# Value products in split fp32r form, in groups of four heads, in the last loop of a two-block fp32 kernel

## The reference

```
u = rmsnorm_2(h); proj = u @ w_in
# 16 MLA heads (latent q and kv, rope) and 16 "fox" heads (forget gate), head size 64
s = q @ k.T * scale (+ cum[t] - cum[s] for fox), causal mask over 272 keys
p = softmax(s)                      # per head, 256 real query rows
out = einsum('bhqk,bhkd->bhqd', p, v)
o_mla * silu(z_mla) @ w_br_mla,  o_fox * silu(z_fox) @ w_br_fox
mixed = (sigmoid(gate_a) * y_mla + sigmoid(gate_b) * y_fox) @ w_out
h = h + rmsnorm_2(mixed)
```

## Time and profile before

| | us |
|---|---|
| median of 3 runs | 955.57 |
| profiled execution, whole | 956.61 |
| its span in the trace | 954.8 |
| PE busy | 930.5 (97%) |
| DVE busy | 580.2 (61%) |
| ACT busy | 479.3 (50%) |
| POOL busy | 38.8 (4%) |
| the last loop | about 647 to 899 |

### The profile page before, as it was taken

The page is one execution under the profiler, slowest core; times in us unless marked ns, Lnnn a source line. Parts: engine busy times, 40 slices in busy tenths (PEclk is TensorE's granted clock), DMA queues, the critical chain, the costliest instruction groups (busy, mean ns, idle before and its releaser), DMA issues.

```text
span 954.8 us, 13629 instructions
## 1 busy us (share of the span) xinstructions
PE 930.5 (97%) x5017; PEld 775.3 (81%) x5017; DVE 580.2 (61%) x1061; ACT 479.3 (50%) x773; POOL 38.8 (4%) x67
## 2 busy tenths in 40 slices
PE   6999999999999999999999999999999999999996
PEld 6877778888888899878888888889987878878775
DVE  5866857646355578567355453776665565565565
ACT  6565566344353547556353443686354445445442
POOL 1013200000000000000000000001011000000000
PEclk9999999999999999999999999999999999999998
DMA  8542256554635522236645546232433242433541
GB/s 304 213 177 89 93 190 220 196 201 147 238 142 213 184 89 90 89 131 242 223 152 199 196 153 238 94 134 80 189 101 127 100 161 89 177 132 132 174 158 44
DMA packets 26375, 150.43 MB, mean 158 GB/s; under 512 B 3664, under 2 KB 3920, under 8 KB 12112
## 3 DMA queue, kind: packets, MB, share of 16 engines
q1 hardware_dynamic: 24912, 147.44, 42.3%
q0 software_dynamic: 1408, 2.25, 0.8%
HBM read 148.50 MB, written 1.05 MB: 157 GB/s over the span
## 4 chain that ended last, share of the span: by engine, by line
PE 83%; DVE 8%; ACT 4%; DMA 2%; issue 2%; DVEq 1%; ACTq 0%; SPq 0%
PE bank L472 24%; PE bank L473 23%; PE bank L474 23%; DVE w_lo L1830 2%; DMA w_raw<-w_main_dram 2%; PE bank L543 1%; PE bank L1033 1%; PE bank L752 1%; DVE arena L2217 1%; PE bank L1048 1%; PE bank L1086 1%; PE bank L890 1%; PE bank L1068 1%; PE bank L1069 1%; PE bank L866 1%
## 5 line engine op out<-in xcount | busy, mean ns | idle before, releaser
L472 PE MATMUL bank<-w_hi,x_hi 128*128 128x512 f32 (+2 forms) x640 | 259.7, 406 | 1.3 <-DVE w_lo L1738 0.8
L473 PE MATMUL bank<-w_lo,x_hi 128*128 128x512 f32 (+2 forms) x640 | 249.9, 390 | 0.0
L474 PE MATMUL bank<-w_hi,x_lo 128*128 128x512 f32 (+2 forms) x640 | 249.5, 390 | 0.0
L1738 DVE TENSOR_TENSOR w_lo<-w_raw,w_hi 128x2048 fp32r<-128x2048 f32 x50 | 114.5, 2292 | 75.3 <-ACT w_hi L1219 74.3
L472 PEld LDWEIGHTS bank<-w_hi,x_hi 128*128 128x128 f32 x640 | 120.6, 188 | 30.0 <-issue 4.1
L474 PEld LDWEIGHTS bank<-w_hi,x_lo 128*128 128x128 f32 x640 | 120.2, 188 | 27.4
L1219 ACT ACTIVATE w_hi<-w_raw 128x2048 fp32r<-128x2048 f32 x54 | 103.4, 1918 | 76.9 <-DMA w_raw<-w_main_dram 70.9
L473 PEld LDWEIGHTS bank<-w_lo,x_hi 128*128 128x128 f32 x640 | 120.6, 188 | 22.3
L1830 DVE TENSOR_TENSOR w_lo<-w_raw,w_hi 128x2048 fp32r<-128x2048 f32 x51 | 116.2, 2284 | 5.0 <-ACT w_hi L1280 4.8
L1280 ACT ACTIVATE w_hi<-w_raw 128x2048 fp32r<-128x2048 f32 x50 | 94.8, 1906 | 14.6 <-DMA w_raw<-w_main_dram 14.1
L472 PE MATMUL bank<-x_hi,w_hi 128*128 128x256 f32 (+1 forms) x272 | 80.4, 296 | 9.0 <-DVE w_lo L1840 8.4
(11 more groups left out here) (372 smaller groups left out, 1460.4 us busy)
## 6 DMA issues: line engine op xcount, KB each, us to landing
w_raw<-w_main_dram SPq DMA_DIRECT2D x111, 1024.0 KB, 4.9
s_raw<-w_side_dram SPq DMA_DIRECT2D x51, 512.0 KB, 4.2
w_raw<-w_main_dram SPq DMA_DIRECT2D x2, 512.0 KB, 6.5
h<-x_dram SPq DMA_DIRECT2D x2, 512.0 KB, 10.7
arena<-rows_dram POOLq DMA_DIRECT2D x2, 512.0 KB, 4.1
arena<-x_t_dram SPq DMA_DIRECT2D x1, 768.0 KB, 7.0
out_dram<-arena SPq DMA_DIRECT2D x1, 512.0 KB, 2.6
out_dram<-arena SPq DMA_DIRECT2D x2, 256.0 KB, 2.1
```

What stands on the lines that cost most here:

```text
L472: pe.matmul(out, ah, bh, start=first, stop=False)
L473: pe.matmul(out, ah, bl, start=False, stop=False)
L474: return pe.matmul(out, al, bh, start=False, stop=last)
L1738: dve.tensor_tensor(w_lo[:, slot, 4 * g:4 * g + 4, :], w_raw[:, g, :, :], w_hi[:, slot, 4 * g:4 * g + 4, :], ALU.subtract).then_inc(w_lo_o ...
```

## The change

Each value product becomes two fp32r matmuls in place of one fp32 matmul. The transposed probabilities are split: ACT copies bank 5 to `hi` as fp32r, DVE writes `lo` = bank 5 - `hi`, in place of DVE's copy. GpSimd splits the 64 value columns of each head into `[v_hi | v_lo]`, side by side. One matmul takes `hi` against all 128 columns, one takes `lo` against the 64 of `v_hi`. A head now takes 128 columns of a bank, so a bank holds four heads (QUAD), and the meta turns, meta products and `group_out` come eight times, at n = 4, 8, 12, ..., 28 and 31; `group_out` first adds the two halves (`tensor_reduce`) and then scales. The meta product has 4 x 64 columns in place of 512.

The tiles of `hi` and `lo` lie in `s_hi`, `s_lo` for the MLA heads and in `g_hi`, `g_lo` for fox. So that these are free, the splits of the side units of `w_uq` move from the end of turns 1 and 5 to turns 4 and 8, between the new ACT copy and `head_exps(n + 2)` on ACT, and between the new subtraction and `head_masked(n + 2)` on DVE; `mla_query` of turns 5 and 9 goes behind the first rider half. `o_mla` moves to another place in SBUF, and some fox turns by one.

```diff
-FOX_TURNS = {RIDERS.index([("gb", 0, 1)]) + j: (2 * j, 2 * j + 1) for j in range(2)}
+FOX_TURNS = {RIDERS.index([("gb", 0, 1)]) + 2 * j: (2 * j, 2 * j + 1) for j in range(2)}
-GROUP_ENDS = {GROUP: 0, 2 * GROUP: 1, 3 * GROUP: 2, 2 * NH - 1: 3}
+QUAD = 4
+QUAD_ENDS = {QUAD * (g + 1) if g < 7 else 2 * NH - 1: g for g in range(8)}
...
+        def head_tiles(n):
+            if n >= NH:
+                return g_hi[:, 2 * P + M:5 * P + M], g_lo[:, M:3 * P + M], g_lo[:, 3 * P + M:5 * P + M].rearrange(...)
+            slot = 0 if 4 <= n < 8 else 1
+            return (s_hi[:, slot, 0:3 * P], s_lo[:, slot, 0:3 * P],
+                    s_hi[:, slot, 3 * P:5 * P].rearrange("p (k e) -> p k e", k=2))
...
# GpSimd
+            for n in range(2 * NH):
+                pool.wait_ge(pt_ps, A2 + n + 1)
...
+                v = (v_m if n < NH else f_v)[:, :, n % NH * HD:(n % NH + 1) * HD]
+                pair = head_tiles(n)[2]
+                hi, lo = pair[:, :, 0:HD], pair[:, :, HD:2 * HD]
+                pool.tensor_copy(hi, v)
+                pool.drain()
+                pool.tensor_tensor(lo, v, hi, ALU.subtract).then_inc(vs_ok, 1)
+                if n in (8, 9, 12, 13):
...
# PE
-                pe.matmul(bank[6][:, at], pt[:, 0:P], v(0), start=first, stop=False)
-                pe.matmul(bank[7][:, at], pt[:, P:2 * P], v(0), start=first, stop=False)
-                pe.matmul(bank[7][:, at], pt[:, 2 * P:3 * P], v(1), start=False, stop=False)
+                for b, i, kt in ((bank[6], 0, 0), (bank[7], 1, 0), (bank[7], 2, 1)):
+                    v_ = v[:, kt if n < NH else 1 - kt, :]
+                    pe.matmul(b[:, a:a + 2 * HD], hi[:, i * P:(i + 1) * P], v_, start=first and kt == 0, stop=False)
+                    pe.matmul(b[:, a:a + HD], lo[:, i * P:(i + 1) * P], v_[:, 0:HD], start=False, stop=False)
...
-                    ins = pe.matmul(bank[6 + r][:, :], pt[:, 384 + r * P:384 + (r + 1) * P], meta_v[g], start=False, stop=True)
+                    ins = pe.matmul(halves(bank[6 + r], 0), pt[:, 384 + r * P:384 + (r + 1) * P], meta_v[g], start=False, stop=True)
...
-                if n + 3 < NH:
+                if n + 3 < NH and n not in (5, 9):
                     mla_query(n + 3)
...
                     riders(RIDERS[n], 0)
+                if n in (5, 9):
+                    mla_query(n + 3)
# ACT
+                act.wait_ge(pt_ps, A2 + n + 1)
+                act.activation(head_tiles(n)[0], bank[5][:, 0:384], ACT.Copy).then_inc(ph_ok, 1)
+                if n in (4, 8):
+                    act.wait_ge(uq_ps, n + 1)
+                    split_side(U_Q + 1 + n // 4)
...
                 if n + 2 < NH or n in FOX_PAIRS:
                     head_exps(n + 2)
-                if n in GROUP_ENDS and n < 2 * NH - 1:
-                    meta_turned(GROUP_ENDS[n])
+                if n in QUAD_ENDS and n < 2 * NH - 1:
+                    meta_turned(QUAD_ENDS[n])
...
-                if n in (1, 5):
-                    act.wait_ge(uq_ps, n // 4 * 4 + 1)
-                    split_side(U_Q + 2 + n // 4)
# DVE
-                dve.wait_ge(pt_ps, A2 + n + 1)
-                dve.tensor_copy(pt[:, 0:384], bank[5][:, 0:384]).then_inc(pt_ok, 1)
+                dve.wait_ge(ph_ok, n + 1)
+                hi, lo, _ = head_tiles(n)
+                dve.tensor_tensor(lo, bank[5][:, 0:384], hi, ALU.subtract).then_inc(pt_ok, 1)
+                if n in (4, 8):
+                    rest_side(U_Q + 1 + n // 4)
...
-                if n in (1, 5):
-                    rest_side(U_Q + 2 + n // 4)
...
+                    ins = dve.tensor_reduce(rows[r], bank[6 + r][:, :].rearrange("p (a f e) -> p a e f", a=QUAD, f=2), AX, ALU.add)
                 ins.then_inc(og_ok, 1)
+                dve.drain()
+                for r in range(R):
+                    roots = root_p[:, r, g % 2 * QUAD:(g % 2 + 1) * QUAD]
+                    dve.tensor_tensor(rows[r], rows[r], roots.rearrange(...).to_broadcast([P, QUAD, HD]), ALU.mult)
```

More of the change, by code:

```diff
@@ L458, in _ @@
                 pool.dma_start(both(v_mm[a * M:(a + 1) * M, :])[:, :, own], both(vu_rows)[:, :, own]).then_inc(um_landed, 16)
[L459 to L464, removed]
+            pool.wait_ge(hx_ok, 1)
+            pool.memset(meta_p[0][:, :, QUAD * M:], 0.0)
+            pool.memset(meta_p[1][:, :, 0:QUAD * M], 0.0).then_inc(blank_ok, 1)
+            for t in range(2):
+                for cc in range(2):
+                    n = USE[("uv", 1 + t, cc)]
+                    pool.wait_ge(acc_free[n % 2], n // 2 + 1)
+            for n in range(2 * NH):
+                pool.wait_ge(pt_ps, A2 + n + 1)
+                if n == NH:
+                    for c in range(2):
+                        for t in (1, 2):
+                            i = USE[("fv", c, t)]
+                            pool.wait_ge(acc_free[i % 2], i // 2 + 1)
+                    pool.wait_ge(sc_ps, A2 + NH)
+                    pool.memset(meta_p[2][:, :, QUAD * M:], 0.0)
+                    pool.memset(meta_p[3][:, :, 0:QUAD * M], 0.0).then_inc(blank_ok, 1)
+                v = (v_m if n < NH else f_v)[:, :, n % NH * HD:(n % NH + 1) * HD]
[5 more added lines that the diff above has]
+                if n in (8, 9, 12, 13):
+                    c, half = (n - 8) // 4, n % 2
+                    pool.wait_ge(vm_ok, c + 1)
+                    for a in range(half * QUAD, (half + 1) * QUAD):
+                        own = slice(a * HD, (a + 1) * HD)
+                        pool.dma_start(f_vm[a * M:(a + 1) * M, c * CH:(c + 1) * CH][:, own], vf_rows[c][:, own]).then_inc(fm_landed[c], 16)
+            pool.wait_ge(og_ok, 8)
             pool.dma_start(row_g, rows[1]).then_inc(rowg_landed[1], 16)
@@ L1157, in _ @@
                     st_wait("o_mla", KT // 2 - 1)
-                last = n % GROUP == 0 and n // GROUP
+                last = n % QUAD == 0 and n // QUAD
                 if n:
                     riders(RIDERS[n], 0)
+                if n in (5, 9):
+                    mla_query(n + 3)
                 if last:
@@ L2473, in _ @@
                         rest_half(c, c % 2, g)
-                if n and n % GROUP == 0:
-                    group_out(n // GROUP - 1)
+                if n and n % QUAD == 0:
+                    group_out(n // QUAD - 1)
                 if len(keys) == 2:
```

67 lines of the change are left out of this document (32 added, 35 removed).

## The result

| | before | after |
|---|---|---|
| median of 4 runs, us | 955.98 | 968.41 (967.07 to 969.95) |
| ratio to before | | 1.013, interval 1.0118 to 1.0142 |
| profiled execution, its span | 954.8 | 966.8 |
| T(0) to T(31), 31 turns of the last loop | 239.48 | 251.65 |

The forecast was 965.3 us (+9.7) with 958 to 970; +12.4 was measured, 2.7 more (the median before is now 955.98, of four runs). Here T(n) of the kernel after is the start of L1097, the same third transpose.

What follows compares the result with a forecast made beforehand. PE was taken to bound the kernel, busy 251.1 of 252.0 us in the last loop. Terms 0 + 0.9 + 6.1 + 1.5 + 1.0 + 0.2 = +9.7 gave 965.3 us against the median, with 958 to 970 holding eight in ten.

Steps and rivals of the forecast that it cites:

- value products: PE's products per head: six loads of 0.107 us make 0.64 us against 0.62 before, counted as 0.
- transposes of four more meta turns: On PE, eight groups in place of four need four more pairs of transposes of 0.11 us: +0.9 us.
- wait in turn 4: PE's first meta product at n = 4 starts at T + 5.7 against 2.9, delayed by copy and side split: +2.8 us.
- turn 1, `w_lo`: Weight halves in turn 1: ACT's copy stands behind the logarithm, so the mask comes later: +1.5 us (0.5 to 2).
- turns 3, 5, 6, `w_lo`: PE's waits for weight halves behind later masks, forecast at turns 4 and 6, move by 0.55 and about 0.45: +1.0 us.
- tail: At the loop's end only two K steps of the next product cover group_out's added scalings: +0.2 us (0 to 1).
- half hidden: Rival on the value products: loads are half hidden, a head costs 0.44 us, -6.4 us, so 959; chance 0.12.
- only the columns: Rival on the value products: loads fully hidden, a head costs 0.24 us, 953.1 us and faster; chance 0.07.
- intervals below 0.09 us between the value products: Sign that the forecast is wrong; it expected loads 0.1 us apart and 0.62 to 0.67 us per head.
- Meta products at n = 4, 8, 12: PE waits for turned meta probabilities delayed by ACT's copy and, at 4 and 8, side splits: +6.1 us (4.5 to 8).
- Contention of DVE and GpSimd: Rival: GpSimd's 1.06 us delays DVE's critical chain at n = 1, 3, 4, 5, 8, 12: +6, so 971; chance 0.10.
- Smaller waits: Rival: side split overlaps better or turn 4's wait is made good later, half of 8.6: 961; chance 0.08.

Runs made afterwards that it cites:

- doubled products: Changed kernel with each product of lo and v_hi issued twice, 96 more fp32r matmuls; 980.03 us, ratio 1.0246.
- 64 columns: Changed kernel with hi against the 64 columns of v_hi alone, as many loads but fewer columns; 968.42 us, ratio 1.013.
- turned first: Changed kernel with ACT's copy of the turned meta probabilities right behind its copy of bank 5, ahead of side split and exponentials; 961.16 us, ratio 1.0055.
- link alone: Kernel before with only ACT's extra copy of bank 5 and a two-input DVE operation waiting for it; 958.87 us, ratio 1.0036.
- filled waits: Two runs of the changed kernel with unread matmuls in PE's waits: turn 4 only, 968.28 us; turns 4, 8 and 12, 967.3 us.
- filled in turn 4: Changed kernel with 11 unread fp32r matmuls of 512 columns on PE before the meta product of turn 4; 968.28 us, ratio 1.0126.
- logs later: Changed kernel with the logarithm of the forget gates at the end of ACT's turn 1 instead of turn 0; 968.06 us, ratio 1.0125.
- side late: Changed kernel with side-unit splits of turns 4 and 8 behind exponentials and turned-probability copy on ACT, behind the mask on DVE; 967.11 us, ratio 1.0115.
- all filled: Changed kernel with unread matmuls before the meta products: 11 in turns 4 and 8, 4 in turn 12; 967.3 us, ratio 1.0117.
- before tuned: Kernel before with the turned meta probabilities copied ahead of the exponentials and the logarithm one turn later; 955.41 us, ratio 0.9992.
- repaired kernel: Changed kernel with turned probabilities copied first, logarithm a turn later, turn 8's reduce ahead of weight halves, ready z half before last group_out; 960.17 us, ratio 1.0041.

## Why the prediction was right, and where its size was off

The sign and the mechanism were right. By its own steps, in the trace after:

| step | predicted | measured | by |
|---|---|---|---|
| value products | 0 | 0 (0.605 us a head for 0.614) | timeline; doubled and narrowed products |
| transposes of four more meta turns | +0.9 | +1.0 (0.22 to 0.25 in each of turns 3, 11, 19, 27) | turns |
| wait in turn 4 | +2.8 | +2.6 | turned first |
| wait in turn 8 | +2.3 | +2.1 (2.62 for 0.49) | turned first |
| wait in turn 12 | +1.0 | +1.0 | turned first |
| turn 1, `w_lo` | +1.5 | +1.36 | link alone (1.32) |
| turns 3, 5, 6, `w_lo` | +1.0 | +0.54 and +0.33 | link alone (0.50 and 0.32) |
| half clock in turn 4 | none | +1.6 | filled waits |
| tail | +0.2 | +0.8 (0 in all, with 0.86 less of meta product) | timeline only |

These make 11.3 of the 12.0 us by which the span grew. Of the rest, 0.2 lies in turn 4 and 0.1 in turn 12, which both went with the waits in *turned first*, and 0.02 to 0.07 in each of many turns. The two half meta products that change places across T(31) (0.86) are in none of the rows.

- *Value products.* The load was the limit, as argued from the earlier trace rows. 96 more products cost 0.11 us each, and the columns of `v_lo` nothing. The rivals *half hidden* (959) and *only the columns* (953) fall with it. One of the prediction's own signs of being wrong did appear: "intervals below 0.09 us between the value products". Inside after's pairs the distances alternate, 0.142 us behind a product of 128 columns and 0.080 behind one of 64, so a pair is 0.222, while the loads start evenly 0.11 apart. The sign was ill chosen; the interval should have been asked of loads, or of pairs. The sum for the four products of the earlier trace rows was off as well: two of 0.107 and two of 272 / 2.4 = 0.113 us make 0.44, not the 0.47 that the chain has, so those rows were weaker support than was claimed. The Trainium skill (TensorE: Matmul & The Clock Gate, section Back-to-back issue gap) gives some 81 ns per matmul at N = 128. This case's 0.111 us a matmul, in pairs of 128 and 64 columns as with 64 in all, isn't that. The same page of the Trainium skill, section LDWEIGHTS, gives a load as its columns over 1.2 GHz, 107 ns for 128. The 0.111 us agree with it to 4%.
- *Waits at the meta products.* Predicted T + 5.7, 5.7 and 3.9, released by L1710; they started at T + 5.6, 5.5 and 3.9, all released by it, and when L1710 was moved up 7.3 us came back. That ACT's copy took 0.489 us for 0.53 is part of why they came a little earlier. PE's idle time in the loop rose to 7.7 us, where "some 9" was the sign.
- *The step that was mis-sized* is "Meta products at n = 4, 8, 12", whose sum +6.1 counted waits as idle time and no more. It measured 7.3: 5.7 of longer waits and 1.6 of work at half clock behind one of them. The prediction had read "all intervals below hold at one clock" from the earlier trace rows, which shows a kernel whose PE is idle for 0.9 us in the whole loop, and the change took just that away. The half clock alone, 1.6 us, is the larger part of the 2.7 us by which the forecast was short. The rest is the tail (0.6) and small errors of both signs.
- *Tail.* The two scalings, 0.76 us, now stand ahead of DVE's product with `half_u`, and PE's next transposes wait for both; the two K steps that were to cover this did so only in part. No run takes the scalings out. The repair of this place left a wait of 0.8 us, for another cause.
- *Contention of DVE and GpSimd* (971): the total came within 2.6 us of it. What rules it out is that DVE's subtraction takes 557 ns with GpSimd beside it, and that the mask starts after GpSimd's two steps in the six turns that were named. The run with the link alone, in which GpSimd has no such steps, shows the same delays (1.32 us in turn 1, 0.50 in turn 3).
- *Smaller waits* (961): no; the `w_lo` waits in turns 3 to 6 were 0.1 us below their terms.

What stays open: which of two like waits draws the half clock. It came in turn 4 (after; 64 columns), in turn 8 (filled in turn 4; logs later), in both (doubled products), in turn 9 (side late) and in neither (all filled, turned first). In the loops of these runs it came only behind an idle stretch of PE, and cost some 1.6 us each time; when it comes I can't say. Whether the earlier start by 0.85 us moved it or each execution draws anew isn't shown either: only one execution of each kernel has a profile, and *turned first* has a half clock far ahead of the loop too, where all twelve kernels are the same and PE has the same waits of some 0.7 and 1.0 us; none of the other eleven profiles has it there:

```profile
113.40:116.70 3.30, 3.30 (x10) 2.51 (x10) 2.07 (x5) 1.70 (x5) 0.00 (x0) 0.50 0.00 0
```

The other four executions of that kernel have a mean clock of 0.997 or 0.998, this one 0.996. Nor is the kernel before free of such draws: among the eleven executions of *before tuned* those with a mean clock of 0.999 took 954.10 to 955.08 us, and those with 0.996 or 0.997 took 955.60 to 956.57.

The 4.0 us by which the repaired kernel's loop is longer are read from its turns only, not tested: 1.0 transposes, 1.4 the link in turns 1, 3, 5 and 6, 0.9 turn 9, and one half meta product more before T(31) (0.86, which the tail gives back but for its wait), less 0.5 for the wait gone from turn 8. These make 3.7; the rest is spread over many turns.

## What to carry to other kernels

Where a stationary of 128 columns meets few moving columns, count loads, not passes or columns: three fp32 products and six fp32r products took the same 0.6 us. A hop added to a link that PE doesn't wait for directly still delays everything queued behind it, so ask for each queue what stands there and who takes it; here 0.5 us of copying in each of 32 turns cost some 3 us (2.7 in the turns of the profile, 3.4 by the ratio). On the engine that feeds PE, put the short copy that PE waits for ahead of the long work for later turns, which gave back 7.3 of 12.4 us; moving the long work back instead can pass the wait on to whatever stands there. And where PE, never idle so far, is first made to wait, reckon with its clock on top of the wait: here it cost 1.6 us.

## What the runs showed of the hardware that I had not expected

- An idle stretch of PE of 2.5 us, and once two of 0.9 and 1.5 us, was followed by some 3 us at the 1.2 GHz level: 13 matmul records in 3.1 us at 0.50, 25 at 1.00. It cost 1.6 us, and came behind one of two waits of the same length, not always the same.
- Of one kernel's executions on one chip, those with a mean clock of 0.999 took at most 955.08 us and those with 0.996 or 0.997 at least 955.60: part of the spread between runs goes with the clock.
- fp32r matmuls with 128-column stationaries came at 0.111 us on average with 64 or 128 moving columns, but in uneven steps (0.142 and 0.080 us) where the widths alternate.
- GpSimd's two steps, 290 and 460 ns on 128x128, left DVE's subtraction of 128x384 from PSUM beside them at 557 ns, the same as without them.
